# Placing the experts' stationary operands group by group, 64 bytes apart round 512

## What is computed

```python
def moe_swiglu(x, router, w1, w3, w2):
    logits = (xt @ router).astype(F32)
    top_v, top_i = lax.top_k(logits, TOP_K)
    gates = jax.nn.softmax(top_v, axis=-1)
    ...
    for e in range(N_EXPERTS):
        h = jax.nn.silu(xt @ w1[e]) * (xt @ w3[e])
        y = y + dense_gate[:, e:e + 1].astype(x.dtype) * (h @ w2[e])
```

## Time and profile before

| | us |
|---|---|
| median of 3 runs | 1288.18 |
| lowest, highest | 1287.72, 1288.54 |
| the profiled execution's span | 1288.5 |
| expert stage in it, first to last fp32r matmul | 522.6 to 1273.4 |

### The profile page before, as it was taken

One profiled execution on the slowest core, in us unless ns is written; L12 is line 12 of the kernel. 1 busy time (PEld: TensorE's weight loads), 2 busy tenths in 40 slices (PEclk: granted clock), 3 DMA queues, 4 the chain that ended last, 5 costly groups with the idle time before them and its releaser, 6 DMA issues.

```text
span 1288.5 us, 17344 instructions
## 1 busy us (share of the span) xinstructions
PE 1247.9 (97%) x5932; PEld 1034.4 (80%) x5932; DVE 1052.9 (82%) x1049; ACT 837.0 (65%) x863; POOL 126.5 (10%) x111
## 2 busy tenths in 40 slices
PE   7999999999999979999999999999999999999995
PEld 6889877888878857778888888888888888888884
DVE  5778885455567988889899889888998998898996
ACT  4565654444524474578777777777777777787772
POOL 1063001000004912200000000000000000000001
PEclk9999999999999999999999999999999999999998
DMA  9653058666436515899999999999999999999991
GB/s 351 221 183 104 14 191 294 196 190 210 141 129 209 174 49 197 298 382 384 389 380 387 389 380 387 389 380 387 389 381 382 389 380 381 388 369 376 390 370 53
DMA packets 195058, 374.76 MB, mean 291 GB/s; under 512 B 9392, under 2 KB 27952, under 8 KB 194880
## 3 DMA queue, kind: packets, MB, share of 16 engines
q1 hardware_dynamic: 189072, 351.37, 76.8%
q0 software_dynamic: 5936, 22.74, 4.8%
HBM read 363.07 MB, written 11.01 MB: 290 GB/s over the span
## 4 chain that ended last, share of the span: by engine, by line
PE 90%; DVE 5%; DMA 2%; ACT 1%; issue 1%; POOL 0%; SPq 0%; DVEq 0%; ACTq 0%
PE psum L390 22%; PE psum L392 22%; PE psum L391 22%; PE psum L411 4%; PE psum L412 4%; PE psum L413 4%; PE psum L2040 1%; DMA raw<-in_od_w 1%; DVE wlo L381 1%; PE psum L1572 1%; PE psum L1571 1%; PE psum L1570 1%; PE psum L1712 1%; PE psum L1594 1%; PE psum L1596 1%
## 5 line engine op out<-in xcount | busy, mean ns | idle before, releaser
L381 DVE TENSOR_TENSOR wlo<-raw,whi 128x1536 fp32r<-128x1536 f32 (+1 forms) x426 | 676.6, 1622 | 137.9 <-ACT whi L375 136.8
L375 ACT CAST whi<-raw 128x1536 fp32r<-128x1536 f32 (+1 forms) x426 | 581.8, 1376 | 212.6 <-PE psum L392 176.2
L390 PE MATMUL psum<-whi,xe_hi 128*128 128x512 f32 x704 | 277.8, 395 | 2.8 <-DVE wlo L381 2.5
L392 PE MATMUL psum<-whi,xe_lo 128*128 128x512 f32 x704 | 274.6, 390 | 0.0
L391 PE MATMUL psum<-wlo,xe_hi 128*128 128x512 f32 x704 | 274.1, 389 | 0.0
L390 PEld LDWEIGHTS psum<-whi,xe_hi 128*128 128x128 f32 x704 | 132.2, 188 | 31.2 <-DVE wlo L381 4.2
L392 PEld LDWEIGHTS psum<-whi,xe_lo 128*128 128x128 f32 x704 | 132.1, 188 | 28.1
L391 PEld LDWEIGHTS psum<-wlo,xe_hi 128*128 128x128 f32 x704 | 132.3, 188 | 26.5
L390 PE MATMUL psum<-whi,hTe_hi 128*128 128x512 f32 x352 | 138.4, 393 | 0.0
L392 PE MATMUL psum<-whi,hTe_lo 128*128 128x512 f32 x352 | 137.2, 390 | 0.0
L391 PE MATMUL psum<-wlo,hTe_hi 128*128 128x512 f32 x352 | 137.1, 389 | 0.0
(11 more groups left out here) (333 smaller groups left out, 1482.5 us busy)
## 6 DMA issues: line engine op xcount, KB each, us to landing
raw<-in_od_w SPq DMA_DIRECT2D x262, 768.0 KB, 9.8
raw<-in_od_w SPq DMA_DIRECT2D x95, 512.0 KB, 9.4
raw<-in_ev_w SPq DMA_DIRECT2D x33, 768.0 KB, 4.4
raw<-in_ev_w_in SPq DMA_DIRECT2D x32, 512.0 KB, 6.6
raw<-in_od_w_in SPq DMA_DIRECT2D x24, 512.0 KB, 4.6
raw<-in_od_w SPq DMA_DIRECT2D x32, 384.0 KB, 8.0
raw<-in_ev_w SPq DMA_DIRECT2D x12, 512.0 KB, 3.8
raw<-in_od_w SPq DMA_DIRECT2D x24, 256.0 KB, 7.6
```

Of the source, the lines that this page charges most:

```text
L375: nc.scalar.copy((whi if into is None else into)[i % GT][:, 0:n], src[:, 0:n]).then_inc(hi_done, 1)
L381: nc.vector.tensor_tensor((wlo if into is None else into)[i % GT][:, 0:n], src[:, 0:n], (whi if high is None else high)[i % GT][:, 0:n].bi ...
L390: nc.tensor.matmul(ps, hi, w_h[:, r, :], start=start, stop=False)
L392: ins = nc.tensor.matmul(ps, lo, w_h[:, r, :], start=False, stop=stop)
```

## The change

The stationary operands of the experts are split into the groups in which they are evicted: `xe` into two pairs (high part, rest), `hTe` into six. Each pair begins 64 bytes further than the end of the pair ahead of it, so that round 512 the pairs stand at 64 and 128 (`xe`) and at 192, 256, 320, 384, 448 and 0 (`hTe`). The high part and the rest of one group have the same phase, since a group is a multiple of 512 bytes. `h_e` moves ahead of `xe` and keeps phase 0. All that follows stands 512 bytes further and keeps its phase, but for `rows`, which goes from 0 to 64. `xT_f`, which the router reads (line 1970), goes from 0 to 128. Instructions, their order, sizes and waits are those of before on every engine; the operands' addresses alone differ.

```diff
--- before.py
+++ after.py
@@ -31,6 +31,7 @@
 FF = 2816
 KF = FF // P
 NE = 8
+STEP = 64
 EVEN_IN, ODD_IN = 4096, 3072
 QA, ZF, ZB, VA, GA, QB, KB, VB = (512 * i for i in range(8))
 DEPTH = 2
@@ -119,6 +120,7 @@
         sem = lambda name: ctx.enter_context(nc.semaphore(name))
 
 
+        TURNS = [(0, 4, 6, 1), (4, 4, 7, 2), (8, 4, 6, 3), (12, 4, 7, 4), (16, 4, 6, 5), (20, 2, 3, None)]
         base = (nc.sbuf_base + 63) // 64 * 64
         top = nc.sbuf_usable_end
         cur = [base]
@@ -219,11 +221,19 @@
 
 
         xn, m2 = at("xn", [P, NT, D], F32, after_gains)
-        xe_hi, m3 = at("xe_hi", [P, KD, P], F32R, m2)
-        xe_lo, m4 = at("xe_lo", [P, KD, P], F32R, m3)
-        h_e, m5 = at("h_e", [P, FF], F32, m4)
-        hTe_hi, m6 = at("hTe_hi", [P, KF, P], F32R, m5)
-        hTe_lo, m7 = at("hTe_lo", [P, KF, P], F32R, m6)
+        h_e, m3 = at("h_e", [P, FF], F32, m2)
+
+        def stepped(name, sizes, offset, first):
+            pairs = []
+            for g, kc in enumerate(sizes):
+                start = offset + (STEP if g or first else 0)
+                hi, o = at(f"{name}_hi{g}", [P, kc, P], F32R, start)
+                lo, offset = at(f"{name}_lo{g}", [P, kc, P], F32R, o)
+                pairs.append((hi, lo))
+            return pairs, offset
+
+        xe, m5 = stepped("xe", (4, 4), m3, True)
+        hTe, m7 = stepped("hTe", [kc for _, kc, _, _ in TURNS], m5, True)
         silu_e, m8 = at("silu_e", [P, 2, NB], F32, m7)
         pick, m9 = at("pick", [P, NT, P], F32, m8)
         put, m11 = at("put", [P, S], F32R, m9)
@@ -461,7 +471,6 @@
 
 
 
-        TURNS = [(0, 4, 6, 1), (4, 4, 7, 2), (8, 4, 6, 3), (12, 4, 7, 4), (16, 4, 6, 5), (20, 2, 3, None)]
         TURN_AFTER = {after: g for g, (_, _, _, after) in enumerate(TURNS) if after is not None}
         ROWS_AFTER, PLACE_AFTER = 2, 1
 
@@ -916,7 +925,7 @@
             def gather_hi(n):
                 for b in range(2):
                     act.wait_ge(m_ga, 2 * n + b + 1)
-                    nc.scalar.copy(xe_hi[:, 4 * b:4 * b + 4, :].rearrange("p k s -> p (k s)"), psum[:, 4 + b, :]).then_inc(m_ga_hi, 1)
+                    nc.scalar.copy(xe[b][0][:].rearrange("p k s -> p (k s)"), psum[:, 4 + b, :]).then_inc(m_ga_hi, 1)
 
             def keep_map(n):
 
@@ -927,7 +936,7 @@
             def turn_hi(n, g):
                 k0, kc, bank, _ = TURNS[g]
                 act.wait_ge(m_tp, 6 * n + g + 1)
-                nc.scalar.copy(hTe_hi[:, k0:k0 + kc, :].rearrange("p k s -> p (k s)"), psum[:, bank, 0:kc * P]).then_inc(m_thi, 1)
+                nc.scalar.copy(hTe[g][0][:].rearrange("p k s -> p (k s)"), psum[:, bank, 0:kc * P]).then_inc(m_thi, 1)
 
             def high_parts(n, tiles, last, again):
 
@@ -1402,17 +1411,14 @@
             def gather_lo(n, bs=range(2)):
                 for b in bs:
                     dve.wait_ge(m_ga_hi, 2 * n + b + 1)
-                    dst = slice(4 * b, 4 * b + 4)
-                    nc.vector.tensor_tensor(xe_lo[:, dst, :].rearrange("p k s -> p (k s)"), psum[:, 4 + b, :],
-                                            xe_hi[:, dst, :].rearrange("p k s -> p (k s)").bitcast(F32),
-                                            ALU.subtract).then_inc(m_ga_lo, 1)
+                    nc.vector.tensor_tensor(xe[b][1][:].rearrange("p k s -> p (k s)"), psum[:, 4 + b, :],
+                                            xe[b][0][:].rearrange("p k s -> p (k s)").bitcast(F32), ALU.subtract).then_inc(m_ga_lo, 1)
 
             def turn_lo(n, g):
                 k0, kc, bank, _ = TURNS[g]
                 dve.wait_ge(m_thi, 6 * n + g + 1)
-                nc.vector.tensor_tensor(hTe_lo[:, k0:k0 + kc, :].rearrange("p k s -> p (k s)"), psum[:, bank, 0:kc * P],
-                                        hTe_hi[:, k0:k0 + kc, :].rearrange("p k s -> p (k s)").bitcast(F32),
-                                        ALU.subtract).then_inc(m_tlo, 1)
+                nc.vector.tensor_tensor(hTe[g][1][:].rearrange("p k s -> p (k s)"), psum[:, bank, 0:kc * P],
+                                        hTe[g][0][:].rearrange("p k s -> p (k s)").bitcast(F32), ALU.subtract).then_inc(m_tlo, 1)
 
             def low_parts(n, tiles, last=False, end=False):
 
@@ -2053,11 +2059,11 @@
 
                 k0, kc = UP_ROWS[i]
                 bank = 2 * (i // 6 % 2) + (i // 3 % 2 if i < UP_END[-2] else 0)
-                return [[(psum[:, bank, :], xe_hi[:, k, :], xe_lo[:, k, :], k == 0, k == KD - 1)] for k in range(k0, k0 + kc)]
+                return [[(psum[:, bank, :], *(part[:, k % 4, :] for part in xe[k // 4]), k == 0, k == KD - 1)] for k in range(k0, k0 + kc)]
 
             def down_rows(i):
 
-                return [[(psum[:, 2 * half, :], hTe_hi[:, k, :], hTe_lo[:, k, :], k == 0, k == KF - 1)] for half, k in DN_ROWS[i - N_UP]]
+                return [[(psum[:, 2 * half, :], *(part[:, k % 4, :] for part in hTe[k // 4]), k == 0, k == KF - 1)] for half, k in DN_ROWS[i - N_UP]]
 
             def block_e(n, b):
                 pe.wait_ge(m_h, UB * n + b + 1)
```

## The result

The change makes the kernel slower: 1302.07 us (median of 4 runs, 1300.43 to 1302.62) against 1288.36 us for before in the same set. The ratio is 1.0105, interval 1.0093 to 1.0117. The forecast was no change, 1288.2 us, with a range to 1292.0, so it was wrong. The time came out near that of the slower rival (1305 us).

The account below looks back on a forecast made before the run. The prediction took the always-supplied TensorE, through the distance between the experts' fp32r matmul starts, to bound the kernel. All terms were 0, so 1288.5 + 0 us, or 1288.2 us against the median, range 1284.5 to 1292 us.

Parts of the forecast that it names:

- slower rival: Experts' slices across two 512-byte stretches need another read: 3072 matmuls at 5.5 ns, 16.9 us more, 1305 us; chance 0.11.
- What bounds the kernel, and the lever of 3.2 us per ns: TensorE bounds the experts' stage; 3168 fp32r matmuls make one nanosecond of distance between starts worth 3.2 us.
- The base of the sum: Starting time of the forecast: the profiled execution's 1288.5 us, read as one with the median of 1288.18 us.
- Loads of the stationary operand: Experts' loads, mostly across two 512-byte stretches after the change, take 188 to 190 ns, covered by 39 ns: cost 0.
- Stationary and moving operand read at the same time: In the experts' matmuls, different phases of the two operands leave the distance unchanged, judged from fp32 rows: cost 0.
- the open point: Experts: no fp32r matmul in the trace has operands at different phases; the slower and the faster rival both live there.
- The constant surplus as a fixed price: fp32r matmuls take 13 ns beyond their columns at 256 and 512 alike, a price no address changes: 0.
- Evictions: ACT and DVE writes of `xe` and `hTe` banks don't disturb the stream; any change hides in waits: cost 0.
- The tail: Behind each group's four transposes, nine distances are 5.5 ns longer; gone or doubled, 2.4 us either way; value 0.
- What moves along: `rows` at phase 64 costs 0, `xT_f` in 32 small matmuls under 0.1 us, `h_e` keeps its phase.
- The Trainium skill: Documentation's rule that TensorE never waits for anyone in SBUF, so no placement helps or hurts; its 216 ns gap was rejected.
- The faster rival: Experts' fp32r stream: equal phases disturb its reads; new phases save up to 10 ns each, 1256.5 us at best; chance 0.11.

Follow-up runs that it names:

- the kernel with steps of 256: The changed kernel, split into groups as it is, with each pair offset by 256 bytes in place of 64: 1288.97 us, ratio 0.9998 against before.
- the one run that took the surplus away: The kernel before with the moving operand of the experts' fp32r matmuls read as one element 512 times (output differs): 1284.36 us, before 1289.10.

## Why the prediction was wrong, by its steps

- **What bounds the kernel, and the lever of 3.2 us per ns**: right. Mean distances over the stage rose from 227.4 to 232.7 ns in `xe` and from 227.1 to 230.5 in `hTe`: 2112 x 5.3 + 1056 x 3.4 ns = 14.8 us. Some of it is taken back in the first expert: from its first matmul on `xe` to that of the second expert it takes 96.36 us after, only 0.3 us more than the 96.09 us of the kernel with steps of 256, whose stream is as fast as before, and TensorE waits 0.6 us for `wlo` in it instead of 1.6. 13.7 us are left. (In the profile of before the first expert took 97.25 us with 2.5 us of that wait.)
- **The base of the sum**: misread, without consequence. The profiled span, 1288.5 us, was taken for the same thing as the median time, 1288.18 us. In every later run the span is 1.8 to 1.9 us shorter than the time of the same execution, so the profiled execution of before took, by my estimate from these, some 1290.3 us.
- **Loads of the stationary operand**: right. Their mean is 188 to 190 ns at every phase, and lying across two stretches costs nothing. The slower rival's price of 5.5 ns on 3072 matmuls, 16.9 us, was near the truth by luck (14.8 us by the distances), since its mechanism was not: it took the price from the tail behind transposes and the reason from the load.
- **Stationary and moving operand read at the same time**: here is the step that failed. I put this term at 0; it is 5.3 ns in `xe` and 3.4 ns in `hTe`, all of the loss. I took 0 because fp32 rows at mixed phases showed nothing, and those rows stand unchanged in every run (216 ns on line 1669 with the moving `lev` at 0 and `sA` at 384). But they were the wrong witness: in fp32 a column takes about two cycles. The fp32r stream reads about twice as fast (0.12 us for 256 columns) and reacts; the fp32 rows show the relations 0 and 384 only, and that the rate is the reason isn't shown. I had named this as the open point, and gave it 0.22 for both signs, as if a lack of rows were weak evidence for no effect.
- **The constant surplus as a fixed price**: wrong. 13 ns at 256 and at 512 columns looked like a price per matmul. The moving operand that stands still takes 10.9 of them away, and with 256 columns the phase moves the distance too (last section). Why the surplus is alike at both lengths with all at phase 0 is open.
- **Evictions**: right, 0; no run shows one that disturbs the stream. **The tail** of 232 ns behind transposes was a hint that I priced and didn't read: its distance is near that of the slow phases, so an fp32r stream with nothing to wait for can run slower, and the one at phase 0 falls into its fast rhythm within some ten matmuls. That both have one cause isn't shown. I listed it under evictions, as something that the change could mend.
- **What moves along**: right, by the kernel with steps of 256, but for `xT_f`, which is at 0 there and so isn't tested by it.
- **The Trainium skill**: the rule of "SBUF — State Buffer", "Who interferes with whom", that TensorE never waits for anyone, stands beside a table that lists its two read ports as independent; in these runs the distance of fp32r matmuls depends on the addresses of both reads. On its two read ports "TensorE: Matmul & The Clock Gate", "Step-by-step: what each phase is for", says that loading the next tile's weights doesn't steal read bandwidth from the running matmul. For fp32r that doesn't hold here: the distance depends on where the two operands stand to each other (226.7, 228.9 or 233.3 ns for the relations 0, -64 and 64), and a moving operand that stands still has 215.8 ns.
- **The faster rival**: its room of 10 ns exists, but its mechanism has the sign wrong, since equal phases are the best ones for 512 columns. Its best case of 1256.5 us was not reached either: in the one run that took the surplus away the loads left 4.7 us. I had seen that floor and not put it into the price.

## What to carry to other kernels

Where a dense stream of fp32r matmuls bounds a kernel, the byte address of the stationary slice less that of the moving operand is a setting with a price: keep it a multiple of 256 for 512 columns, as these runs have it, and after any change of the layout look at the distance between matmul starts, which shows 1 to 3% at once while all durations stay. A row of another type is no witness for this one, however much it looks like it: when the only rows at hand differ in the rate at which they read, the effect is unknown, not absent.

## What the runs showed of the hardware

- Most settled distances come in even steps if three are taken together: on average 680 ns (3 x 226.7), 686.7 (228.9), 693.3 (231.1) or 700 (233.3). A step is 6.67 ns, 16 columns or 64 bytes of the stream. Single distances in the slow rhythms go from 224 to 241 ns, and 234.4 ns (`xe` at 96) lies on no step. What sets the number of these steps is not known, and the relation alone doesn't: 16 bytes allow 226.7 and 233.3 ns.
- Which of the relations 0 and 64 is the faster depends on the length of the stream. With the stationary slice at 64 and the moving one at 0, 256 columns of fp32r (the first layer's gates, in the run with `x` and `xT` at 64) start every 1.36 us / 12 = 113 ns, where 0 has 120 ns. This holds in four of the seven groups of these matmuls; in the other three it is 118 ns. The same relation is bad for 512 columns.

```profile
...
113.70 0.28 PE L1685 MATMUL psum<-lev,xT_lo 128*128 128x256 f32 x1
...
115.06 0.28 PE L1685 MATMUL psum<-lev,xT_lo 128*128 128x256 f32 x1
```

- A stationary operand read as one element 128 times has no faster stream than a swept one (means of 229.9 and 229.6 ns, where the kernel before has 227.4 and 227.1), a moving one has 215.8 ns when settled.
